# Gate and up projections channel by token in a fused two-layer kernel

## The reference

```
h = rmsnorm(x, ffn_norm_w)                                 # 256 x 2048
x = x + (silu(h @ w_gate) * (h @ w_up)) @ w_down           # 2048 -> 5632 -> 2048
return rmsnorm(x, final_norm_w)
```

## Time and profile before

| what | value |
|---|---|
| median of 3 runs | 2382.64 us (2382.16 to 2382.72) |
| profiled execution | 2382.65 us |
| its span | 2380.8 us |
| instructions | 28492 |
| granted clock of TensorE, mean | 0.999 |
| TensorE busy | 99% of the span |
| VectorE busy, ScalarE busy | 60%, 50% |
| DMA traffic | 430.81 MB, 181 GB/s in the mean |

### The profile page before, as it was taken

How to read it: one execution, slowest core, us unless ns; L and a number is a source line. 1 busy time by engine, 2 the same in 40 slices (tenths; PEclk the granted TensorE clock), 3 DMA queues, 4 the chain that set the end, 5 groups by cost and what they waited for, 6 DMA issues and landing times.

```text
span 2380.8 us, 28492 instructions
## 1 busy us (share of the span) xinstructions
PE 2364.4 (99%) x11458; PEld 1938.3 (81%) x11458; DVE 1425.4 (60%) x1701; ACT 1184.1 (50%) x1695; POOL 241.6 (10%) x336
## 2 busy tenths in 40 slices
PE   9999999999999999999999999999999999999998
PEld 7888888888788888888887778788888888888886
DVE  5655665665566545665864565576554554557775
ACT  6544453454445444555645455465444444446654
POOL 0053004305300430000000010000000000000000
PEclk9999999999999999999999999999999999999999
DMA  6565457446535655666665454456555555555554
GB/s 211 194 174 164 142 177 186 155 156 182 171 127 187 177 165 168 221 207 198 209 218 191 142 179 146 155 178 226 188 187 194 189 184 193 194 181 192 193 195 141
DMA packets 240658, 430.81 MB, mean 181 GB/s; under 512 B 32180, under 2 KB 35133, under 8 KB 240526
## 3 DMA queue, kind: packets, MB, share of 16 engines
q1 hardware_dynamic: 227536, 413.38, 54.4%
q10 hardware_dynamic: 12990, 15.60, 2.1%
HBM read 423.66 MB, written 5.29 MB: 180 GB/s over the span
## 4 chain that ended last, share of the span: by engine, by line
PE 89%; POOL 5%; DVE 2%; DMA 1%; issue 1%; ACT 1%; ACTq 0%; SPq 0%; POOLq 0%; DVEq 0%
PE gemm L1311 27%; PE gemm L1313 27%; PE gemm L1312 27%; POOL arena L2264 5%; PE side L893 3%; DMA arena<-delta_blocks 1%; DVE arena L1732 1%; DVE weight_lo L1726 1%; PE side L1234 1%; PE side L981 0%; PE side L903 0%; PE side L1249 0%; PE side L1273 0%; ACT weight_hi L1339 0%; PE side L1047 0%
## 5 line engine op out<-in xcount | busy, mean ns | idle before, releaser
L1726 DVE TENSOR_TENSOR weight_lo<-weight_raw,weight_hi 128x1024 fp32r<-128x1024 f32 x780 | 969.7, 1246 | 733.5 <-ACT weight_hi L1339 732.2
L1339 ACT ACTIVATE weight_hi<-weight_raw 128x1024 fp32r<-128x1024 f32 x780 | 821.9, 1056 | 860.9 <-PE gemm L1313 820.3
L1311 PE MATMUL gemm<-weight_hi,x_hi 128*128 128x512 f32 x2368 | 942.1, 398 | 3.3 <-DVE x_lo L1732 2.1
L1313 PE MATMUL gemm<-weight_hi,x_lo 128*128 128x512 f32 x2368 | 923.1, 390 | 0.0
L1312 PE MATMUL gemm<-weight_lo,x_hi 128*128 128x512 f32 x2368 | 922.1, 389 | 0.0
L1311 PEld LDWEIGHTS gemm<-weight_hi,x_hi 128*128 128x128 f32 x2368 | 444.7, 188 | 103.4 <-issue 12.5
L1313 PEld LDWEIGHTS gemm<-weight_hi,x_lo 128*128 128x128 f32 x2368 | 444.4, 188 | 94.3
L1312 PEld LDWEIGHTS gemm<-weight_lo,x_hi 128*128 128x128 f32 x2368 | 445.1, 188 | 89.4 <-issue 1.4
L1311 PE MATMUL gemm<-weight_hi,lhs_hi 128*128 128x512 f32 x736 | 287.1, 390 | 0.0
L1313 PE MATMUL gemm<-weight_hi,lhs_lo 128*128 128x512 f32 x736 | 286.4, 389 | 0.0
L1312 PE MATMUL gemm<-weight_lo,lhs_hi 128*128 128x512 f32 x736 | 286.3, 389 | 0.0
(11 more groups left out here) (184 smaller groups left out, 1028.4 us busy)
## 6 DMA issues: line engine op xcount, KB each, us to landing
weight_raw<-in_w_in_dram SPq DMA_DIRECT2D x207, 1024.0 KB, 5.1
weight_raw<-in_w_out_dram SPq DMA_DIRECT2D x48, 1024.0 KB, 5.1
weight_raw<-in_w_gate_dram SPq DMA_DIRECT2D x44, 1024.0 KB, 5.2
weight_raw<-in_w_up_dram SPq DMA_DIRECT2D x44, 1024.0 KB, 5.2
weight_raw<-in_w_down_dram SPq DMA_DIRECT2D x44, 1024.0 KB, 5.0
arena<-rel_line ACTq DMA_DIRECT2D x8, 384.0 KB, 6.1
arena<-in_x_dram SPq DMA_DIRECT2D x4, 512.0 KB, 9.5
arena<-delta_blocks ACTq DMA_DIRECT2D x16, 128.0 KB, 5.2
```

Of the source, the lines that this page charges most:

```text
L1311: e.matmul(pair[i][:, :], xh[:, s], wh, start=first, stop=False)
L1313: m = e.matmul(pair[i][:, :], xl[:, s], wh, start=False, stop=last)
L1339: return e.activation(o, i, ACT.Copy, scale=scale)
L1726: return e.tensor_tensor(o, x, y, op)
```

## The change

For the jobs fg and fu (`ACROSS`) the operands change places: 128 columns of weights stand and 256 tokens move. A job's 512 channels are four quarters q of 128, two in each bank of the pair, 256 columns apart. The first matmul of a bank is 512 columns wide and moves k-row 0 with a block of zeros behind it (`xhi` gets a 17th row of zeros, made at the start), so that the whole bank is opened at once.

The result is channel by token, as `d` wants it: `fturn` and its copies go. The norm's factor now has to multiply along the row: `rdiag` scales the identity by r for each token tile, `rrow` multiplies ones by it on TensorE and copies the result to `rrows` (128 equal rows of 256 factors). `fgate` (VectorE) writes gate * r to z, `tanh` works on z from SBUF, `silu` is one operation on 1024 columns, `fact` is two operations (z/2 * up) and one (times r) that writes `acts_all`. The bank pair of fg is given free by `fgate`, that of fu by the first part of `fact`.

```
+ACROSS = ["fg", "fu"]
...
+    if kind == "fg":
+        return [("dve:fgate", number_of(name))]
...
+            put(s + 5, "rdiag", "r2"), put(s + 6, "rrow", "r2")
     for n in range(FFN // NC):
-        put(END[f"fg{n}"], "tanh", f"fg{n}"), put(END[f"fg{n}"] + 1, "silu", f"fg{n}")
-        s = END[f"fu{n}"]
-        put(s, "fact", n), put(s + 1, "fturn", n, 0), put(s + 1, "fturn", n, 2)
+        put(END[f"fg{n}"], "fgate", n), put(END[f"fg{n}"], "tanh", f"fg{n}"), put(END[f"fg{n}"] + 2, "silu", f"fg{n}")
+        put(END[f"fu{n}"], "fact", n)
...
-        def fturn(n, c):
-            w.wait_ge(*at("dve:fact", n))
-            p = open_bank("fturn", n, c)
-            turn_pair(p, blk("z", f"fg{n}"), c).then_inc(sem("pe:fturn"))
+        def rrow(tag):
+            w.wait_ge(*at("dve:rdiag", tag))
+            p, d = open_bank("rrow", tag), blk("diag", tag)
+            for i in range(NT):
+                m = e.matmul(p[:, i * P:(i + 1) * P], ONE, d[:, i * P:(i + 1) * P], start=True, stop=True)
+            m.then_inc(sem("pe:rrow"))
...
+                if kind_of(name) in ACROSS:
+                    for q in range(NC // P):
+                        o, s = pair[q // 2][:, q % 2 * T:(q % 2 + 1) * T], slice(q * P, (q + 1) * P)
+                        if first and q % 2 == 0:
+                            e.matmul(pair[q // 2][:, :], wh[:, s], xhi[:, 0:KD + 1:KD, :], start=True, stop=False)
+                        else:
+                            e.matmul(o, wh[:, s], xh, start=False, stop=False)
+                        e.matmul(o, wh[:, s], xl, start=False, stop=False)
+                        m = e.matmul(o, wl[:, s], xh, start=False, stop=last and q % 2 == 1)
+                    continue
...
         def tanh(key):
+            if kind_of(key) == "fg":
+                th = claim("th", key)
+                w.wait_ge(*at("dve:fgate", number_of(key)))
+                e.activation(th, blk("z", key), ACT.Tanh, scale=0.5).then_inc(sem("act:tanh"))
+                return
...
+            w.wait_ge(sem("dve:zeros"), 1)
+            e.tensor_copy(xhi[:, KD, :], xfer[:, 0:T])
...
+        def rdiag(tag):
+            d = claim("diag", tag)
+            w.wait_ge(*at("dve:nscale", tag))
+            for i in range(NT):
+                s = ts(d[:, i * P:(i + 1) * P], IDN, scale_of(tag)[0][:, i:i + 1], ALU.mult)
+            s.then_inc(sem("dve:rdiag"))
...
+            if kind_of(key) == "fg":
+                stt(b, blk("th", key), 1.0, b, ALU.add, ALU.mult).then_inc(sem("dve:silu"))
+                return
...
+        def fgate(n):
+            z = claim("z", f"fg{n}")
+            w.wait_ge(*at("dve:rrow", "r2"))
+            w.wait_ge(*out_of(f"fg{n}"))
+            for i in range(2):
+                s = tt(by_row(part(z, i)), by_row(pair_of(f"fg{n}")[i][:, :]), over(rrows[:, :], 1, 2), ALU.mult)
+            s.then_inc(sem("dve:fgate"))
...
         def fact(n):
...
-            for i in range(NT):
-                s = stt(part(g, i), part(g, i), sq[:, i:i + 1], pair_of(f"fu{n}")[i][:, :], ALU.mult, ALU.mult)
+            for i in range(2):
+                s = stt(part(z, i), part(z, i), 0.5, pair_of(f"fu{n}")[i][:, :], ALU.mult, ALU.mult)
             s.then_inc(sem("dve:fact"))
...
+            w.wait_ge(*at("dve:fact:u", n))
+            tt(acts_all[:, 4 * n:4 * n + 4, :], by_row(z, 4), over(rrows[:, :], 1, 4), ALU.mult).then_inc(sem("dve:fact"))
```

More of the change, by code:

```diff
@@ L373 @@
 STAGES = {
-    "norm": ("cols0", "cols", "xturn", "sqsum", "nscale"),
+    "norm": ("cols0", "cols", "xturn", "sqsum", "nscale", "rdiag", "rrow"),
     "kept": ("kept",), "gate": ("tanh", "silu", "mgate"),
@@ L394 @@
             "dY": ("",), "donorm": ("mean", ""), "mscore": ("w", "den"), "msq": ("mean", ""),
-            "gsum": ("end", "rest", ""), "gstate": ("first", ""), "gsq": ("mean", ""), "alog": ("b", "")},
+            "gsum": ("end", "rest", ""), "fact": ("u", ""), "gstate": ("first", ""), "gsq": ("mean", ""), "alog": ("b", "")},
     "pool": {"dinv": ("zero", "")},
@@ L398 @@
 for _engine, _names in {
[L399 to L400 removed]
+        "pe": "cols0 cols xturn rrow gate1 fsum rel1 convturn dnorm dsc dT dX dv du0 dbu du1 do dout chan mdec mscore "
+              "mturn mnum mout ggate2 gsum gscore gkend gstate go gout alog aturn apv",
         "act": "xturn sqsum kept tanh convtap convsilu dnorm dT du0 du1 donorm dout chan mexp mturn msq mout "
[L402 to L405, removed]
+               "ggabs ggexp ggln gkend gsq gout aexp aturn apv",
+        "dve": "cols xturn rdiag rrow kept silu gate0 gate2 fsum rel0 rel1 convtap convsilu ddecay dsc dX dv dbu do "
+               "dgate mdec mm mden mgate mgated yb yhalf ya yres x1w gload ggate0 ggate2 ggate3 gscore ggated anorm res2 res4 fgate "
+               "fweight",
         "pool": "nscale dss drhs dmask donorm dgate mrhs msq gsq anorm tail"}.items():
@@ L458, in block_table @@
             last = {"mo": ("dve:mgate", n), "dz": ("dve:dgate", n), "mz": ("dve:mgated", n), "gb": ("dve:yhalf", n),
-                    "ga": ("dve:yres", n), "gr": ("dve:ggated", n), "fg": ("pe:fturn", n, 2)}[kind]
-            live(("z", key), ("tanh", key), last)
+                    "ga": ("dve:yres", n), "gr": ("dve:ggated", n), "fg": ("dve:fact", n)}[kind]
+            live(("z", key), ("fgate", n) if kind == "fg" else ("tanh", key), last)
     live(("nar", "gates"), ("gate0",), ("pe:gate1",))
@@ L513, in block_table @@
             live(("ET", half, c), ("aturn", half, c), ("pe:apv", half, c))
+    for n in range(FFN // NC):
+        live(("th", f"fg{n}"), ("tanh", f"fg{n}"), ("dve:silu", f"fg{n}"))
+    live(("diag", "r2"), ("rdiag", "r2"), ("pe:rrow", "r2"))
     for z in range(3):
-        live(("tail", z), ("fturn", 8, 0), home=z)
+        live(("tail", z), ("fact", 8), home=z)
     return t
@@ L614, in _build @@
     llo = sb("lhs_lo", [P, LRING, 2, T], F32R)
[L615 removed]
+    xhi = sb("x_hi", [P, KD + 1, T], F32R)
     xlo = sb("x_lo", [P, KD, T], F32R)
@@ L1664, in x2load @@
             load(by_tile(x), x2_dram[:, :, n * NC:(n + 1) * NC], f"dma:x2load{n}")
-        def fturn(n, c):
-            if c:
-                return
-            if n == 8:
-                for z in range(3):
-                    claim("tail", z)
-            w.wait_ge(sem("pe:gemm"), END["o3"])
-            w.wait_ge(*at("pe:fturn", n, c))
-            copy(acts_all[:, 4 * n:4 * n + 2, :], by_head(bank("fturn", n, c), 2)).then_inc(sem("act:fturn"))
         def tail(i):
@@ L1776, in nscale, with rrow, by_row @@
                 after(tt(r, r, scale_of("r1")[0], ALU.mult))
-            if tag == "r2":
-                sq = stat(NT, "ffn scale")
-                after(ts(hr, r, 0.5, ALU.mult))
-                tt(sq, hr, r, ALU.mult).then_inc(sem("dve:nscale"))
-            else:
-                ts(hr, r, 0.5, ALU.mult).then_inc(sem("dve:nscale"))
+            ts(hr, r, 0.5, ALU.mult).then_inc(sem("dve:nscale"))
+        def rdiag(tag):
[4 more added lines that the diff above has]
+            s.then_inc(sem("dve:rdiag"))
+        def rrow(tag):
+            w.wait_ge(*at("pe:rrow", tag))
+            e.tensor_copy(rrows[:, :], bank("rrow", tag)[:, 0:T]).then_inc(sem("dve:rrow"))
+        def by_row(ap, n=2):
+            return ap.rearrange("p (c t) -> p c t", c=n)
         def kept(key):
@@ L2248, in vector_program @@
                      gscore=gscore, gstate=gstate, gsq=gsq, ggated=ggated, alog=alog, anorm=anorm, res2=res2, res4=res4,
-                     fact=fact, fturn=fturn, fweight=fweight, tail=tail)
+                     rdiag=rdiag, rrow=rrow, fgate=fgate, fact=fact, fweight=fweight, tail=tail)
         for slot in range(-AHEAD, NH + 2):
```

36 lines of the change are left out of this document (13 added, 23 removed).

## The result

The kernel after takes 2405.44 us (median of 4 runs, 2404.72 to 2407.05), the one before 2382.68 us (4 runs, 2382.16 to 2382.75). The ratio is 1.0097, with a 95% interval of 1.0085 to 1.0109: 22.8 us slower. The prediction was 2378.2 us, and the time lies just beyond the range's upper end. The profiled execution took 2405.36 us with a span of 2403.6, against 2380.8 before, so its trace shows the whole difference.

What follows compares the result with a forecast made beforehand. TensorE's matmul count times start-to-start distance, plus inserted side work, was taken to bound the kernel. 4.99 - 10.00 + 0.26 + 0.34 = -4.4 us from 2382.64 gave 2378.2 us, range 2374 to 2403.

Steps and rivals of the forecast that it cites:

- The products: Gate and up matmuls: 4224 of 256 columns at 113.3 ns cost the same 478.7 us as 2112 at 226.7.
- The sentence on the skill: A fixed part of about 2.5 ns per warm matmul would add 5.3 us for 2112 more, ending at 2383.5.
- The opening: First matmul of each bank in fg and fu stays 512 wide, half on zeros: 44 x 113.3 ns, +4.99 us.
- The turns: Eight transposes in each of 11 groups go: -9.60 us, and -0.40 us for the slower stretch behind them.
- The factor as a row: rrow puts two F32 matmuls of 128 columns into TensorE's order once: at most +0.26 us, with no wait.
- slow halves behind bursts: Halves behind two u3 transpose bursts and rrow slow by 5.8 ns a matmul (119.1 less 113.3): +0.34 us.
- VectorE and ScalarE: VectorE's longer group work, 25.2 us of 44, stays hidden; ScalarE loses two PSUM reads and a copy, gains one pass.
- Rival C: Longer VectorE and ScalarE steps delay weight splits, 0.9 us a group, making 2388 us; chance 0.06.
- the tight place at d0: First down job: the activation split, two halves ahead, ends at 2136.2, before its use at 2136.86; 0.6 us to spare.
- A: Gate and up matmuls all keep the slow 119.1 ns: +24.5 us, 2402.7; full or most 0.17, a part 0.13.
- B: Weight loads are not hidden: each of 2112 more costs 0.11 us, +232 us, 2610 us; chance 0.02.
- D: More is won: gate and up matmuls fall to the turns' 109 ns, -18 us, 2360, or smaller gains; chance 0.10.

Runs made afterwards that it cites:

- experiment 1: Separate kernel of blocks of 96 matmuls, one shape each, nothing of the computation: F32R with 128-column weights 119.9 ns at 256 columns, 227.0 at 512.
- experiment 2: Second separate kernel, other column counts and bursts of four F32 matmuls: 320 columns 146.8 ns, 224 columns 111.8; a burst 0.91 or 0.89 us in all.
- experiment 7: Separate kernel, blocks of 96 F32R matmuls of 256 columns, operand places varied: narrow weights side by side 113.3 ns, 32 columns lying 128 apart 117.7, 128 columns 120.0.
- experiment 4: Kernel before with only the fg and fu operands swapped and 256-column openings, turns left in: 2408.78 us, ratio 1.0108.
- experiment 5: Kernel before with each 512-column fg and fu matmul cut into two of 256, orientation kept: 2409.89 us, ratio 1.0112.
- experiment 6: Kernel after with each bank opened by a 256-column matmul of its first quarter instead of 512 columns: 2400.04 us, ratio to before 1.0071.
- experiment 3: Kernel before without the turns' eight transposes per group, copies reading the untransposed product: 2371.83 us, ratio 0.9954.

## Why the prediction was wrong

*What bounds the kernel*: right. The stream of matmuls sets the time, the distance from start to start is what to read, and nothing else came into the path.

*The products*: this step failed. It says: "That is half of 226.7 to the digit, so a matmul shows no part that is paid for each instruction." There is such a part, 13.3 ns for F32R with 128 columns of weights (experiments 1 and 2): 226.7 is 213.3 + 13.4, and 256 columns cost 106.7 + 13.3 = 120.0. The 113.3 of the earlier trace rows is 106.7 + 6.6, with narrow weights lying side by side (experiment 7). Two points with different weights were laid on one line, and it went through zero by accident. The term "nothing" is 2112 more matmuls x 13.3 ns = +28.1 us; experiment 4 measured 25.6, experiment 5 27.4, both 27.1 from the start of the stage on. The other argument, that a load of 128 columns fits under 113 ns, held: its floor is 111 to 112. But it answered another question. That no load stands in the way does not make the stream cost columns / clock.

The sign was in the earlier trace rows themselves. Their 119.1 is a mean; one row more of the kernel before, to be read with the last row:

```profile
43.99 0.28 PE L1307 MATMUL gemm<-x_lo,weight_hi 128*48 128x256 f32 x1
```

The first ten steps, from 42.81 on, are 118 ns, the last twelve, to 45.43, are 120.0. So the spacing does not fall back to 113.3 as the burst recedes, it settles at 120.0, and to choose 113.3 because the stage has no burst inside had no ground. Why this job runs at 113.3 in the half ahead of its burst and at 120.0 behind it, no run shows.

The sentence on the skill (TensorE: Matmul & The Clock Gate, "Back-to-back issue gap") had the right form, columns / 2.4 GHz and a fixed part, and was set aside for the equal ratio. Its 2.5 ns are what bf16 shows here (162.5 ns at 384 columns, 215.8 at 512, inside the blocks); for F32R the runs show five times as much.

*The opening*: +4.99 predicted; 44 x 0.11 = 4.8 us in the trace, 5.4 in the runs of experiment 6 and 4.6 in its trace. Right.

*The turns*: -10.0 predicted, -11.4 measured, with an interval that holds it, and 10.0 from the start of the stage on (experiment 3). Right. The burst of experiment 2 cost the same 0.91 us in all.

*The factor as a row*: +0.26 predicted. TensorE's loads around it, in the timeline of the kernel after:

```profile
1660.93 0.54 PEld L1285 LDWEIGHTS side<-arena,constants 128*128 128x128 f32 x4
...
1661.39 0.19 PEld L1321 LDWEIGHTS gemm<-x_hi,weight_hi 128*128 128x128 f32 x1
```

0.46 us, not 0.26, since each F32 matmul of `rrow` runs as two records. No wait before it. The +0.34 us for slow halves behind bursts rested on the 5.8 ns of the earlier trace rows; experiment 2 shows at most 0.02 us behind each.

*VectorE and ScalarE*: hidden, as worked out. What they wait for in the stage (us in total, times, longest):

```profile
ACT arena L1422 <- DVE arena L1737: 34.6, 11, 3.2
...
DVE arena L1737 <- PE gemm L1323: 5.7, 11, 0.6
```

ScalarE waits 3.1 us each time for VectorE's product before its tanh. VectorE waits 0.5 us in the mean for TensorE's last product before it evicts, so it is not late, and TensorE waits for none of it. Rival C is out, the tight place at d0 included.

*The sum of what the runs showed*: +28.1 + 4.8 - 10.0 + 0.5 = 23.4, against 22.8 measured.

*The rivals*: A was close in its number (119.1 for 120.0 ns, 2402.7 for 2405.4 us), and right that the slow spacing needs no burst. Its reason, twice as many loads in a time, does not hold: the same 13.3 ns are paid at 384 and 512 columns, where a load has far more time. And it is not something that a burst starts: 256 columns with 128 columns of weights take 119.9 ns without one. B is out: 120 ns for load and stream together leave no room for 0.11 us of load in line. D is out: the 109 ns between transposes lie near the floor of 111 to 112, which 256 columns do not reach. With the fixed part known, the change pays only if the turns cost more than 28.1 + 4.8 + 0.5 = 33.4 us, 3.0 us a group; they cost 0.9.

## What to carry to other kernels

To get the price of an instruction from a trace, take two sizes of the *same* form, operands and widths alike, and solve for the fixed part; a ratio between rows of different forms can be exact and mean nothing. Count steps inside one run of equal matmuls and not across its seam, where a record can be missing or start early. Turning a product round to save transposes pays only if the fixed part of the matmuls that it adds is less than they cost: here 2.6 us a group against 0.9. Where types are mixed, keep equal ones together in long runs: the same matmuls in another order were worth 13 us of 2390.

## What the runs showed of the hardware

- ns from start to start by moving columns, 128 columns of weights. F32R: 111.1 (128), 111.3 (160), 111.9 (192), 111.8 (224), 119.9 (256), 131.7 (288), 146.8 (320), 173.3 (384), 203.8 (448), 227.0 (512). bf16, inside the blocks: 55.8 (128), 109.2 (256), 162.5 (384), 215.8 (512), which is columns / 2.4 GHz + 2.5.
- F32 matmuls run as two records each, 215.8 ns a record at 256 columns and 429.2 at 512: 3.6 to 3.8 times the price of F32R.
- Narrow weights do not always help: at 512 columns 64-column weights take 229.9 ns, 128-column ones 227.0.
- A bank needs no zeros for its second half: in experiment 6 the one start flag, on a matmul of 256 columns, opened all of it, and the output stayed the reference's.
- With 64 moving columns, F32R, the granted clock fell in both kernels that had such a block, with the engine never idle. Two windows of the block in experiment 1, columns as above:

```profile
78.70:81.00 2.30, 2.30 (x23) 2.30 (x22) 0.00 (x0) 0.00 (x0) 0.00 (x0) 1.00 0.00 0
83.00:95.90 12.90, 12.90 (x62) 12.90 (x62) 0.00 (x0) 0.00 (x0) 0.00 (x0) 0.50 0.00 1
```

The block starts at full clock (2.4 GHz) with a matmul every 111 ns, as with 128 columns, and goes on at 1.2 GHz with one every 213 ns: the floor doubles when the clock halves. Over the block a matmul took 180 ns, more than one of four times as many columns. The stage in the kernels before and after shows full clock throughout.
